# Two transformer layers on one core: the second layer's attention with zero-padded keys and values, weights rounded in halves

## What is computed

```python
q = rms_norm(q.reshape(B, T, 8, 64), q_norm)
ks, kw = rms_norm(ks, k_norm[1]), rms_norm(kw, k_norm[2])      # 2 groups of 64 each
p_cmp = masked_softmax(q @ kc.T * scale, ...)                  # 31 compressed keys
p_sel = masked_softmax(q @ ks.T * scale, causal)               # selected keys: here all up to t
p_win = masked_softmax(q @ kw.T * scale, causal)               # window of 512: here all up to t
o_nsa = g0 * p_cmp @ vc + g1 * p_sel @ vs + g2 * p_win @ vw
x = x + concatenate([o_nsa, o_hgrn]) @ w_out_2
x = x + (silu(h @ w_gate) * (h @ w_up)) @ w_down
```

## Time and profile before

| | |
|---|---|
| runs | 1542.06, 1540.63, 1539.97 us |
| profiled execution, first to last instruction | 1539.1 us |
| mean granted TensorE clock | 0.983 |
| TensorE busy | 96% |
| VectorE, ScalarE, GpSimd busy | 47%, 35%, 12% |
| DMA | 119.63 MB, 78 GB/s on average |

### The profile page before, as it was taken

The page is one execution under the profiler, slowest core; times in us unless marked ns, Lnnn a source line. Parts: engine busy times, 40 slices in busy tenths (PEclk is TensorE's granted clock), DMA queues, the critical chain, the costliest instruction groups (busy, mean ns, idle before and its releaser), DMA issues.

```text
span 1539.1 us, 17384 instructions
## 1 busy us (share of the span) xinstructions
PE 1475.6 (96%) x6957; PEld 1130.7 (73%) x6957; DVE 717.5 (47%) x1069; ACT 539.9 (35%) x910; POOL 182.2 (12%) x143
## 2 busy tenths in 40 slices
PE   6899999999999999999899999998997999999999
PEld 4777778766666678877787666566786888888887
DVE  4764444534444445342635566364745343433343
ACT  4553333544334333233424354343323231222221
POOL 0117420013333300000000022121000000000000
PEclk9999999999999999999999999898999999999999
DMA  5122123220010043222431100000231323232222
GB/s 189 63 74 83 55 69 110 83 82 28 28 55 28 28 192 137 90 83 82 136 111 51 55 28 28 1 28 1 98 107 55 110 83 109 83 109 98 94 89 76
DMA packets 20432, 119.63 MB, mean 78 GB/s; under 512 B 2304, under 2 KB 3584, under 8 KB 8192
## 3 DMA queue, kind: packets, MB, share of 16 engines
q1 hardware_dynamic: 19776, 117.47, 21.7%
q10 hardware_dynamic: 576, 1.05, 0.3%
HBM read 113.27 MB, written 4.19 MB: 76 GB/s over the span
## 4 chain that ended last, share of the span: by engine, by line
PE 85%; DVE 7%; ACT 3%; POOL 2%; issue 2%; DMA 0%; SPq 0%; DVEq 0%; ACTq 0%
PE bank L718 82%; POOL arena L1957 2%; PE bank L882 2%; PE bank L1053 1%; PE bank L776 1%; DVE arena L1439 1%; DVE arena L1852 1%; DMA arena<-in_x 0%; DVE wlo L1421 0%; DVE a_lo L1613 0%; ACT whi L1118 0%; ACT arena L1240 0%; DVE arena L1588 0%; ACT L1203 0%; ACT a_hi L1226 0%
## 5 line engine op out<-in xcount | busy, mean ns | idle before, releaser
L718 PE MATMUL bank<-a_hi,whi 128*128 128x512 f32 x848 | 342.1, 403 | 0.7 <-DVE a_lo L1613 0.7
L718 PE MATMUL bank<-a_hi,wlo 128*128 128x512 f32 x848 | 332.1, 392 | 0.0
L718 PE MATMUL bank<-a_lo,whi 128*128 128x512 f32 x848 | 332.0, 392 | 0.0
L718 PE MATMUL bank<-arena 128*64 128x128 f32 (+9 forms) x1496 | 287.0, 328 | 14.3 <-DVE arena L1748 8.9
L1421 DVE TENSOR_TENSOR wlo<-wraw,whi 128x2048 fp32r<-128x2048 f32 (+1 forms) x97 | 223.4, 2303 | 90.5 <-ACT whi L1118 89.9
L1118 ACT ACTIVATE whi<-wraw 128x2048 fp32r<-128x2048 f32 (+1 forms) x97 | 183.6, 1893 | 181.1 <-PE bank L718 180.9
L718 PEld LDWEIGHTS bank<-arena 128*64 128x64 f32 (+2 forms) x1496 | 183.1, 171 | 75.3 <-issue 47.4
L718 PEld LDWEIGHTS bank<-a_hi,whi 128*128 128x128 f32 x848 | 160.3, 189 | 38.3 <-issue 7.1
L718 PEld LDWEIGHTS bank<-a_hi,wlo 128*128 128x128 f32 x848 | 160.0, 189 | 34.3
L718 PEld LDWEIGHTS bank<-a_lo,whi 128*128 128x128 f32 x848 | 160.4, 189 | 31.7 <-issue 1.0
L718 PE MATMUL bank<-whi,a_hi 128*128 128x512 f32 x320 | 128.2, 401 | 5.8 <-DVE a_lo L1903 3.0
(11 more groups left out here) (224 smaller groups left out, 1608.2 us busy)
## 6 DMA issues: line engine op xcount, KB each, us to landing
wraw<-in_wblk SPq DMA_DIRECT2D x93, 1024.0 KB, 4.9
wraw<-in_wblk SPq DMA_DIRECT2D x4, 768.0 KB, 4.4
arena<-in_x SPq DMA_DIRECT2D x4, 512.0 KB, 6.0
arena<-in_x SPq DMA_DIRECT2D x1, 2048.0 KB, 7.8
spill<-arena SPq DMA_DIRECT2D x4, 512.0 KB, 8.9
arena<-spill SPq DMA_DIRECT2D x1, 2048.0 KB, 7.9
out<-arena SPq DMA_DIRECT2D x8, 256.0 KB, 2.0
arena<-in_w1k SPq DMA_DIRECT2D x1, 1024.0 KB, 15.8
```

What stands on the lines that cost most here:

```text
L718: return nc.tensor.matmul(o, lhsT, rhs, start=start, stop=stop, **kw)
```

## The change

The keys of the two branches are kept twice, each time in 128 partitions: `kpad[0]` has the keys of group 0 in the upper 64 and zeros in the rest, `kpad[1]` the keys of group 1 in the lower 64. Logits take all 128 partitions of `qT`. The values are kept as 192 columns (group 0, zeros, group 1), and the stationary operand is a window of 128 of them, so that the product fills 128 partitions, 64 of them with zeros added. Heads are laid out in the bank by (r, g) and no longer by pairs, and the rows of `w_out_2` are permuted to match. The compressed branch is added with eight matmuls of 64 columns. The zeros are written by GpSimd. To make room, `wraw` is halved: every block is loaded, rounded and its rest taken in two pieces of 1024 columns.

```diff
-        wraw = [sb(f"wraw{i}", [P, BLK]) for i in range(2)]
+        wraw = [sb(f"wraw{i}", [P, PIECE]) for i in range(2)]          # PIECE = 1024
+        vpad = sb("vpad", [P, NT, 2, 3 * HD])
-        kT = mem(64, [2, T])
+        kpad = [mem(64, [2, T]), mem(0, [2, T])]
...
             for n in range(NB):
-                if n >= 2:
-                    sp.wait_ge(s_lo, n - 1)
-                cols = width(n)
-                sp.dma_start(wraw[n % 2][:, 0:cols], dram["wblk"][n][:, 0:cols]).then_inc(s_w[n % 2], 16)
+                for i in range(2):
+                    if n >= 1:
+                        sp.wait_ge(s_lo, 2 * n + i - 1)
+                    cols = piece(n, i)
+                    sp.dma_start(wraw[i][:, 0:cols.stop - cols.start], dram["wblk"][n][:, cols]).then_inc(s_w[i], 16)
...  gemm, TensorE
                 if s == 0:
-                    pe.wait_ge(s_hi, n + 1)
-                    pe.wait_ge(s_lo, n + 1)
+                    pe.wait_ge(s_hi, 2 * n + 1)
+                    pe.wait_ge(s_lo, 2 * n + 1)
+                if s == (2 if b["form"] == "feature" else 1):
+                    pe.wait_ge(s_hi, 2 * n + 2)
+                    pe.wait_ge(s_lo, 2 * n + 2)
...  summed
+                            pe.wait_ge(s_pads, 3)
-                        for c in range(4):
-                            mm(out_[:, P * c:P * c + P], vcd[:, c // 2, 2 * (c % 2):2 * (c % 2) + 2, :].rearrange("p a b -> p (a b)"),
-                               cpT[:, qt, c // 2, :], False, False, skip_group_check=True)
+                        for g in range(NG):
+                            for r in range(4):
+                                mm(out_[HD * g:HD * g + HD, P * r:P * r + P], vcd[:, g, r, :], cpT[:, qt, g, :],
+                                   False, False, skip_group_check=True)
-                    o = out_[HD * (h % 2):HD * (h % 2) + HD, P * (h // 2):P * (h // 2) + P]
+                    g, r = divmod(h, 4)
+                    o = out_[:, P * r:P * r + P]
-                        last = mm(o, vst[:, kb, P * b + HD * (h // 4):P * b + HD * (h // 4) + HD],
+                        last = mm(o, vpad[:, kb, b, HD * g:HD * g + P],
...  logits, both forms alike
-                        mm(ps, qT[rows_, r, P * qt:P * qt + P], kT[rows_, :, 0:kend], True, False)
+                        mm(ps, qT[:, r, P * qt:P * qt + P], kpad[g][:, :, 0:kend], True, False)
...  ScalarE: round_weights(n, i) at steps 0 and 2 of block n - 1
-                A(whi[n % 2][:, 0:cols], wraw[n % 2][:, 0:cols], ACT.Copy).then_inc(s_hi, 1)
+                A(whi[n % 2][:, cols], wraw[i][:, 0:cols.stop - cols.start], ACT.Copy).then_inc(s_hi, 1)
...  "kv" tile
-                    A(pair(vst[:, i[0], :]), src[:, :, 1, :], ACT.Copy).then_inc(s_end["S"], 1)
+                    A(vpad[:, i[0], :, 0:HD], src[:, :, 1, 0:HD], ACT.Copy)
+                    A(vpad[:, i[0], :, P:P + HD], src[:, :, 1, HD:P], ACT.Copy).then_inc(s_end["S"], 1)
...  "qkturn" of the keys (i = 4, 5): one activation on 128 partitions becomes two on 64
+                        A(kpad[0][0:HD, i - 4, :], bank[BANK[g]][0:HD, :], ACT.Copy, scale=V("k_norm", i - 3)[0:HD, :])
+                        A(kpad[1][HD:P, i - 4, :], bank[BANK[g]][HD:P, :], ACT.Copy, scale=V("k_norm", i - 3)[HD:P, :])\
+                            .then_inc(s_end["S"], 1)
...  VectorE: rest_of_weights(n, i) at steps 2 and 4 of block n - 1 (before: whole, at step 3)
-                v.tensor_tensor(wlo[n % 2][:, 0:cols], wraw[n % 2][:, 0:cols], f32(whi[n % 2][:, 0:cols]),
+                v.tensor_tensor(wlo[n % 2][:, cols], wraw[i][:, 0:cols.stop - cols.start], f32(whi[n % 2][:, cols]),
...  GpSimd, at step ("pos",)
+                    pool.wait_ge(s_norm, norm_no("mix", NT - 1))
+                    g_.memset(vpad[:, :, :, HD:P], 0.0).then_inc(s_pads, 1)
+                    g_.memset(kpad[0], 0.0).then_inc(s_pads, 1)
+                    g_.memset(kpad[1], 0.0).then_inc(s_pads, 1)
```

More of the change, by code:

```diff
@@ L65 @@
 BLK = 2048
+PIECE = 1024
 def weave(*streams, weights=None):
@@ L620, in width, with piece @@
             return BLOCKS[n]["kn"] * sum(c for _, c in BLOCKS[n]["spans"])
+        def piece(n, i):
+            return slice(PIECE * i, min(PIECE * i + PIECE, width(n)))
         def used_by_pe(n):
@@ L909, in nsa @@
                     g, r = divmod(h, 4)
-                    rows_, kend = slice(HD * g, HD * g + HD), P * (qt + 1)
+                    kend = P * (qt + 1)
                     if u == 0:
@@ L923, in nsa @@
                             ps = nsa_logits(u, b)
-                            mm(ps, qT[rows_, r, P * qt:P * qt + P], kT[rows_, b, 0:kend], True, False)
+                            mm(ps, qT[:, r, P * qt:P * qt + P], kpad[g][:, b, 0:kend], True, False)
                             mm(ps[:, kend - P:kend], identb, after, False, True).then_inc(s_nqk, 1)
@@ L1109, in link, with round_weights @@
                 act.wait_ge(s_ac, chain[0])
-            def round_weights(n):
+            def round_weights(n, i):
                 if n >= NB:
                     return
-                act.wait_ge(s_w[n % 2], 16 * (n // 2 + 1))
-                if n >= 2:
+                act.wait_ge(s_w[i], 16 * (n + 1))
+                if n >= 2 and i == 0:
                     act.wait_ge(*used_by_pe(n - 2))
-                cols = width(n)
-                A(whi[n % 2][:, 0:cols], wraw[n % 2][:, 0:cols], ACT.Copy).then_inc(s_hi, 1)
+                cols = piece(n, i)
+                A(whi[n % 2][:, cols], wraw[i][:, 0:cols.stop - cols.start], ACT.Copy).then_inc(s_hi, 1)
             def round_small(kind):
@@ L1320, in _ @@
                     if s[1] == "dt":
-                        round_weights(0)
+                        for i in range(2):
+                            round_weights(0, i)
                     act.wait_ge(s_tile, DONE[s[2]])
@@ L1360, in _ @@
                 if s[0] == "gemm":
-                    if s[2] == 0:
-                        round_weights(s[1] + 1)
+                    if s[2] in (0, 2):
+                        round_weights(s[1] + 1, s[2] // 2)
                     for g in closed(BLOCKS[s[1]], s[2]):
@@ L1880, in _ @@
                 if s[0] == "small":
-                    rest_of_weights(0) if s[1] == "dt" else lower_bound()
+                    if s[1] == "dt":
+                        for i in range(2):
+                            rest_of_weights(0, i)
+                    else:
+                        lower_bound()
                 if s[0] == "dt":
```

26 lines of the change are left out of this document (15 added, 11 removed).

## The result

The changed kernel takes 1516.2 us (median of 4 runs, 1515.73 to 1518.14) against 1540.3 before (4 runs, 1536.17 to 1542.06): ratio 0.985, 95% interval 0.9834 to 0.9866. The forecast was 1525 with its own range to 1521, the whole range 1511 to 1537: faster as said, by 24.1 us where I had said 15.5. The time lies outside my own range and inside the case of the clock that comes back sooner, which had a chance of 0.18. The profiled spans are 1539.1 and 1513.9 us, 25.2 apart.

A forecast was written before the change was run, and what follows sets the result against it. TensorE, busy 96% of the span, was taken as the bound. Its work falls 23.5 us, less 7 given back and 1 for weight halves: 15.5 us, giving 1525 us; own range 1521 to 1530, whole range 1511 to 1537.

The forecast's parts named there:

- the case of the clock that comes back sooner: Rival: in two 1.2 GHz stretches behind long waits, full-array work regains 2.4 GHz sooner; 3 to 13 us more, chance 0.18.
- The main case: The forecast's own range for the whole kernel, 1521 to 1530 us around 1525, chance 0.52.
- Logits: Second layer's attention: 48 pairs of 64-row passes each lose 0.29 us to shape changes; 13.9 us saved.
- Values: Second layer's weights times values: 320 passes in 48 blocks, 0.275 us saved a block; 13.2 us.
- Compressed branch: Four times, eight full-width passes become sixteen of 64 columns with a change in and out; costs 4.6 us.
- Given back: Second layer's attention: VectorE's work stays, so part of TensorE's saving returns as waits; 7 us, ends 0 and 14.
- Weights in halves: Weight blocks in two pieces: no TensorE waits in dense stretches, changed order on VectorE and ScalarE; 1 us slower.
- The term of the norm between the layers: At that norm, pieces of weight work standing ahead of token work delay it; 1.4 us slower.
- The feed-forward norm's +1.1: At the feed-forward norm, weight pieces ahead of the tokens' work make token 1 and all behind it 1.1 us later.
- Loads exposed: Rival: in 320 value passes, full-width weight loads don't hide under a pass; costs 31 us, 1556, chance 0.05.
- costs not the shapes': Rival: the costs follow any plain float32 operand, so nothing is saved and 4.6 + 1 are added; 1546, chance 0.04.
- VectorE takes it: Rival: VectorE paces the stretch and twice the 7 us or more is given back; 1531 to 1538, chance 0.13.

The follow-up runs named there:

- halves only: The kernel before with only the weights loaded, rounded and their rest taken in two pieces of 1024 columns; 1534.2 us, ratio 0.9967 to before.
- both at 64: The changed kernel with keys and values both taken at 64 again, weights, layout and compressed branch as changed; 1534.9 us, ratio 0.9967 to before.
- before with hout first: The kernel before with only the order altered: level 9 and `hout` each ahead of a late gemm step of the next head's `hf` block; 1523.8 us.
- the last comparison: Changed kernel with first layer's attention at full width and `hout` earlier, 1480.3 us; the same plus compressed branch and level 7 at full width, 1486.1 us.

## Why the prediction was right, and where it was wrong

- **The main case.** 1521 to 1530 wasn't met. The time lies in the whole range because the case of the clock, with a chance of 0.18, was counted into it. What moved the time there is 8 us that my sum put at nothing.
- **Logits, 13.9.** 13.7 (12.4 to 13.7). Right in the step and the size.
- **Values, 13.2.** 11.0 (7.2 to 11.0). Right in the step, the size too large. I had left out the load in front of a block behind a mask (the estimate's twenty passes had no such neighbour), ScalarE's copy between the transposes, and that the 11.0 is measured beside a compressed branch at 64, with which narrow values share changes and an overlap in four places (1.9 us).
- **Compressed branch, -4.6.** The old form against the new, everything else at 64: 190.9 against 193.8, so -2.9; with everything at full width 3.5. Mis-sized: the changes are there as charged, but the two halves of the array overlap for 0.38 us each of four times, 1.5 us. I had written that it isn't excluded and put it at nothing.
- **Work in all.** 191.8 to 169.1: 22.7 us; predicted 22.5 without the low clock's 1. That they agree so well is luck: the errors of two terms cancel, and with pairs told apart otherwise it is 18.6 or 20.8.
- **Given back, -7.** Waits rise by 9.7 (5.7 or 7.8 otherwise), of which 2.6 by *halves only* (2.4 or 2.2), which leaves 3.3 to 7.1. The size is right within that, its parts only in part: the three long waits before `hout` stayed as they were, waits for level operands grew, and ScalarE's copies (lines 1305 and 1307) joined, which I had not named.
- **Weights in halves, -1.** +1.0 at equal clock, +0.7 between runs at the same clock. The term of the norm between the layers was right (1.3 for 1.4). The step that failed is the one that put the dense stretches at 0, because TensorE never waits for a piece there and the two engines have over half their time free: it asked who waits for a piece, not whom it stops while it runs. In the first layer's attention that was GpSimd, 3.9 us. The feed-forward norm's +1.1 didn't show (waits there 13.1 before, 12.6 with halves only). The terms of the start and of the gates weren't looked at by themselves.
- **The clock, 0.** Here the forecast failed. At equal clock the change is 16.3 us and the forecast 15.5; some 8 us are the clock, rival *the clock*. A sign that I had named as being wrong came with it: another number of low-clock stretches, three in the attention and not two. My ground against it ("the waits get slightly longer") was true of the waits and told nothing of the low stretches behind them: two of 13.65 us became 6.8, 3.4 and 3.4. But its own ground, work that fills the array, falls too: *halves only* and *both at 64*, without it, have 0.987 and 0.986 against 0.983 before, and *before with hout first* 0.990. Of the 8 us, some 6 (0.004 of the span) are in *halves only*, and the kernel before reaches 0.987 by itself in a third of its runs. That the long waits set off the long falls is shown in the kernel before: both falls begin in them, and without the waits both are gone, two of 3.4 us behind short waits left. Why a fall lasts 13.65 us in one kernel and 3.4 in another, with nearly the same wait ahead (3.81 and 3.80 us, before and *halves only*), stays open.
- **Loads exposed, costs not the shapes', VectorE takes it.** None of the three. Value passes follow each other at 0.112 and not over 0.160; taking both shapes back cost 18.7 us of time (1534.9 against 1516.2); the waits rose by 9.7 us at most and not by 14; and there is no wait for halves of weights in dense stretches (the gemm steps behind the first layer's attention take 133.9 us in both kernels).

The operations on the weights came nearly as read from the straight line (ScalarE 1035 ns predicted, VectorE 1236; here 1054 and 1296 for the full pieces, VectorE's with those in it that wait for GpSimd):

```profile
L1439 DVE TENSOR_TENSOR wlo<-wraw,whi 128x1024 fp32r<-128x1024 f32 x190 | 244.2, 1296 | 57.8 <-ACT whi L1129 52.6
```

## What to carry to other kernels

Read TensorE by starts: here each change between shapes cost about 0.09 us and its first load besides, and zeros (or a neighbour's columns, if the other rows of the result are not read) were cheaper than the change. The other way out wasn't tried: value passes of two heads that go to the two halves of the result in turn, as the compressed branch's do for a moment. Before counting what a wait costs, look at the granted clock behind it: here an order that took three waits of 1.2 to 3.8 us out of the kernel before gave 17 us. And where an operation is cut or moved, ask which engine can't run beside it.

## What the hardware did that I had not expected

- GpSimd's product of 512 keys: 1.28 us alone, 3.83 when VectorE's rest of a whole block (2.27) stands beside it, though the product's record starts 0.16 us earlier. Which of the two has to wait isn't told by the recorded starts alone: a piece 0.28 us behind a product waited for it.
- Two series of passes to different halves of the result's partitions run side by side: seven starts in 0.38 us, where passes into one half are 0.109 apart (0.76 for seven).
- Low-clock stretches here last 3.4, 6.8, 10.2 or 13.65 us, and the same program has a mean clock of 0.983 in some executions and 0.987 in others, 5 us apart.
- A saving of 3.5 us of TensorE's work (the compressed branch) with 0.2 us of effect, and, in the last comparison, a kernel that is faster at equal clock by 3.5 us, as far as that account goes, and slower in time by 5.8.
